# First feed-forward block in one pass over 512 rows, hidden squares kept on chip, low weight parts written over their ring slots

## The reference

```python
D_MODEL, SEQ, CTX_LEN, MLP_HIDDEN = 1024, 256, 256, 4096

def squared_relu_mlp(h, w1, w2):
    return jnp.square(jax.nn.relu(h @ w1)) @ w2

for i in range(DEPTH):                     # DEPTH == 2
    ...
    x = x + gt1 * y_lat
    x = x + gt2 * squared_relu_mlp(modulate_2(rms_norm(x, norm2_g[i]), sh2, sc2), mlp_w1[i], mlp_w2[i])
    if not last:
        ctx = ctx + mods_c[2] * y_ctx
        ctx = ctx + mods_c[5] * squared_relu_mlp(modulate_2(rms_norm(ctx, norm2_g[i]), mods_c[3], mods_c[4]),
                                                 mlp_w1[i], mlp_w2[i])
```

## Time and profile before

| | us |
|---|---|
| median of 3 runs | 2895.1 (2892.4 to 2897.35) |
| span of the profiled execution | 2890.3 |
| PE busy | 2770.7 (96%) |
| PE weight loads busy | 1973.5 (68%) |
| DVE busy | 1186.3 (41%) |
| ACT busy | 709.9 (25%) |

### The profile page before, as it was taken

The page is one execution under the profiler, slowest core; times in us unless marked ns, Lnnn a source line. Parts: engine busy times, 40 slices in busy tenths (PEclk is TensorE's granted clock), DMA queues, the critical chain, the costliest instruction groups (busy, mean ns, idle before and its releaser), DMA issues.

```text
span 2890.3 us, 49935 instructions
## 1 busy us (share of the span) xinstructions
PE 2770.7 (96%) x22276; PEld 1973.5 (68%) x22276; DVE 1186.3 (41%) x2055; ACT 709.9 (25%) x1136; POOL 48.3 (2%) x39
## 2 busy tenths in 40 slices
PE   8899999999999999999998999999999999998998
PEld 6788997877533333333332756899999965697998
DVE  4667764332301101101101587356555433553554
ACT  2234333131200000000000214334444322211443
POOL 0000000000000000000000000000000000131000
PEclk9899999999999999999999999999999998999999
DMA  8756765544899999999999225265554330010452
GB/s 334 304 182 260 277 259 204 190 175 150 347 373 421 421 420 421 420 421 420 421 412 421 74 97 193 73 262 204 190 182 160 140 117 15 24 54 24 181 184 80
DMA packets 95198, 686.88 MB, mean 238 GB/s; under 512 B 10624, under 2 KB 11776, under 8 KB 11904
## 3 DMA queue, kind: packets, MB, share of 16 engines
q1 hardware_dynamic: 94400, 681.37, 60.5%
q10 hardware_dynamic: 576, 2.25, 0.2%
HBM read 682.52 MB, written 1.05 MB: 237 GB/s over the span
## 4 chain that ended last, share of the span: by engine, by line
PE 86%; DMA 6%; DVE 5%; ACT 2%; issue 1%; SPq 0%; POOL 0%; ACTq 0%; DVEq 0%
PE ps L530 42%; PE ps L2053 15%; PE ps L890 12%; PE ps L801 6%; PE ps L2078 5%; DMA AR<-W 3%; DMA ring<-W 2%; PE ps L543 2%; PE ps L2081 2%; PE ps L776 1%; PE ps L2061 1%; DVE macc L646 0%; DMA XT<-XIN 0%; SPq L3577 0%; ACT AR L1761 0%
## 5 line engine op out<-in xcount | busy, mean ns | idle before, releaser
L2053 PE MATMUL ps<-AR 128*32 128x512 f32 x2904 | 440.1, 593 | 11.6 <-DMA AR<-W 10.2
L530 PE MATMUL ps<-HT,ring 128*128 128x256 f32 (+1 forms) x1696 | 443.4, 422 | 1.7 <-ACT HT L719 1.7
L530 PEld LDWEIGHTS ps<-HT,ring 128*128 128x128 f32 x1696 | 324.2, 193 | 114.5 <-issue 75.0
L530 PE MATMUL ps<-FR,FR 128*128 128x256 f32 x3120 | 387.4, 284 | 0.0
L530 PEld LDWEIGHTS ps<-FR,FR 128*128 128x128 f32 x3120 | 378.7, 192 | 3.0 <-issue 2.9
L872 DVE TENSOR_TENSOR FR<-ring,FR 128x2048 fp32r<-128x2048 f32 x129 | 294.4, 2291 | 164.4 <-ACT FR L856 164.4
L890 PE MATMUL ps<-FR,FR 128*128 128x256 f32 x2832 | 349.0, 283 | 0.0
L890 PEld LDWEIGHTS ps<-FR,FR 128*128 128x128 f32 x2832 | 343.8, 192 | 0.0
L2173 DVE TENSOR_TENSOR AR<-AR,ps 128x256 f32<-128x256 f32 x70 | 29.6, 423 | 678.9 <-ACT AR L2136 361.0
L2053 PE MATMUL ps<-ring,AR 128*32 128x512 f32 x1576 | 288.8, 594 | 5.8 <-DMA ring<-W 3.5
L856 ACT ACTIVATE FR<-ring 128x2048 fp32r<-128x2048 f32 x129 | 244.7, 1908 | 130.9 <-PE ps L890 85.2
(11 more groups left out here) (430 smaller groups left out, 2517.1 us busy)
## 6 DMA issues: line engine op xcount, KB each, us to landing
ring<-W SPq DMA_DIRECT2D x431, 1024.0 KB, 5.8
AR<-W SPq DMA_DIRECT2D x215, 1024.0 KB, 21.0
XT<-XIN ACTq DMA_DIRECT2D x2, 1024.0 KB, 8.7
cst<-CS SPq DMA_DIRECT2D x1, 1859.0 KB, 14.3
out<-XT SPq DMA_DIRECT2D x4, 256.0 KB, 2.2
sml<-SM SPq DMA_DIRECT2D x1, 970.5 KB, 10.3
cst<-CS ACTq DMA_DIRECT2D x1, 129.5 KB, 8.1
sml<-SM ACTq DMA_DIRECT2D x1, 16.0 KB, 5.7
```

The source lines that it names most:

```text
L530: ins = g.matmul(out, l, r, **kw)
L2053: ins = g.matmul(bank.ap[group(i), :], mo.hg[e % 2][:, 4 * h + k, group(t)], w[n][:, k, :], start=j == 0 and k == 0, stop=j == 1 and k == ...
```

## The change

The stage no longer goes twice over the weights. `wide_pe` does all 16 slots of w1 for both halves, then all 16 slots of w2, and each slot is loaded and split once: `SLOTS` falls from 646 to 614. A matmul has 512 columns instead of 256, except in slots 0 and 1, which are used for the latent half first and, after the context norm, for the context half. All squares of the hidden layer stay on chip (`wi.H`, 32 tiles of 128 x 512; their low parts overwrite them, `H_low`, and the high parts pass through five turning buffers). The sums of w2 take all 8 PSUM banks. In the last two slots of w2 PE goes bank by bank over both slots, and DVE adds each bank to `XT` as it comes.

`InPlace` replaces `Splits` here: two buffers hold the high part of a slot (`parts = 2`), and the low part is written over the slot in its ring place (`ring_low` is the ring's memory, seen as fp32r). The place is freed by PE's last matmul on the slot (`used`), no longer by DVE. The 9 background steps stand behind slots 2 to 10 of w1. The norm for `odd_mixer` comes after the whole stage. The second feed-forward (`m1`) is written in a form of its own with the same instructions.

```diff
@@ schedule()
-def early_step(block, c, r):
-    return 1 if block == 0 and c == 0 and r < 23 - ATTENTION_STEPS else 0
+def wide_steps(n):
+    return 1 if 2 <= n < 25 - ATTENTION_STEPS else 0
...
     load("ev_out", 4)
-    for block in range(2):
...
-        for c in range(2 - block):
-            for n in range(17):
-                if n < 16:
-                    ahead(2)
-                if n:
-                    ahead(2)
-                bg.go(early_step(block, c, n))
+    load("m0_1", 2)
+    for n in range(16):
+        load("m0_1" if n < 14 else "m0_2")
+        bg.go(wide_steps(n))
+    load("m0_2", 14)
...
@@ program()
+        class InPlace(Splits):
+            def __init__(self, x, names, fr, get):
+                self.x, self.names, self.parts, self.get = x, names, 2, get
...
+            def pair(self, i):
+                return self.hi[:, i % 2, :], ring_low[:, where[slot(*self.names[i])][0], :]
+            def make_dve(self, g, s, n):
...
+                    s.wait_ge(self.x + ".hi", i)
+                    g.tensor_tensor(low, src, high.bitcast(F32), SUB).then_inc(*s.done(self.x + ".lo", i))
...
-        def mlp_pe(g, s, q, bg):
...
+        def wide_pe(g, s, bg):
...
+            def used(n):
+                return s.done("m0.used", n, frees=(slot(*wi.names[n]),))
+            latent, context = slice(0, 256), slice(256, 512)
+            up(0, latent, 0)
+            down_end("ev.down1")
+            up(1, latent)
+            norm_pe(g, s, "m0", (1,))
+            for n in range(2):
+                up(n, context, 1 if n == 0 else None).then_inc(*used(n))
+            for n in range(2, 16):
+                up(n, slice(0, 512)).then_inc(*used(n))
+                bg.go(wide_steps(n))
+            acc = [counts.take("m0.down", m, keep=True) for m in range(8)]
+            for i in range(14):
+                s.wait_ge("m0.lo", 16 + i).wait_ge("m0.d_lo", i)
+                for kk in range(2):
+                    for m in range(8):
+                        if i + kk == 0:
+                            s.wait_emptied(acc[m])
+                        ins = down(i, kk, m)
+                ins.then_inc(*used(16 + i))
+            for i in (14, 15):
+                s.wait_ge("m0.lo", 16 + i).wait_ge("m0.d_lo", i)
+            for m in range(8):
+                for i in (14, 15):
+                    for kk in range(2):
+                        ins = down(i, kk, m)
+                ins.then_inc(*s.done("m0.bank", m, frees=(slot("m0_2", 14), slot("m0_2", 15)) if m == 7 else ()))
...
+            norm_pe(g, s, "odd")
+        def wide_act(g, s):
...
+            for n in range(16):
+                s.wait_ge("m0.used", n)
+                for h in range(2):
+                    g.activation(wi.H[:, 2 * n + h, :], counts.bank("m0.up", n, h)[:, :], ACT.Relu).then_inc(
+                        *s.done("m0.relu", n, h, empties=("m0.up", n, h)))
+                w.make_act(g, s, n + 3)
...
+            for i in range(16):
+                w.make_act(g, s, min(16 + i + 3, 32))
+                if i + 3 < 16:
+                    hidden(i + 3)
+            s.mark("m0.end")
+            squares_act(g, s, "odd", odd_ready(s), 0)
+            norm_root_act(g, s, "odd", 0)
+            shift_act(g, s, "odd", MN["ada1"][0], 0)
```

More of the change, by code:

```diff
@@ L17 @@
 SLOT = 2048
-SLOTS = 646
+SLOTS = 614
 RING = 5
@@ L455, in program @@
         XT = sb("XT", [128, 2, 8, 256])
+        with ExitStack() as first:
+            HT_low = first.enter_context(nc.sbuf_tensor("HT_low", [128, 8, 512], F32R))
         HT = sb("HT", [128, 8, 512])
@@ new lines, in program, with mlp_pe @@
+        ml.pairs = tuple(x[:, :].rearrange("p (k t) -> p k t", k=8) for x in ml.HS)
+        def mlp_pe(g, s):
+            norm_pe(g, s, "m1")
+            w = Splits("m1", ml.names, ml.fr, PARTS, from_ring)
+            for n in range(17):
+                if n < 16:
+                    i = w.next()
+                    b = counts.take("m1.up", n)
+                    s.wait_emptied(b).wait_ge("m1.lo", i)
+                    if n == 0:
+                        up3_by_k(g, s, "m1", 0, ml.pairs, [
+                            (w.pair(i), 0, b.ap[:, 0:256], True, None),
+                            (w.pair(i), 128, b.ap[:, 256:512], False, lambda: s.done("m1.used", i))])
+                    else:
+                        for h in range(2):
+                            ins = up3(g, w.pair(i), ml.pairs, h * 128, b.ap[:, h * 256:h * 256 + 256])
+                        ins.then_inc(*s.done("m1.used", i))
+                if n == 1:
+                    acc = [counts.take("m1.down0", k, keep=True) for k in range(4)]
+                if n:
+                    i = w.next()
+                    s.wait_ge("m1.lo", i).wait_ge("m1.d_lo", n - 1)
+                    down3(g, s, "m1.down0", w.pair(i), n - 1, 16, acc, [x[:, (n - 1) % 3, :, :] for x in ml.d]).then_inc(*s.done("m1.used", i))
+            down_end("m1.down0")
+            s.mark("m1.end")
@@ new lines, in mlp_act @@
+        def mlp_act(g, s):
+            w = Splits("m1", ml.names, ml.fr, PARTS, from_ring)
+            w.make_act(g, s, 3)
+            norm_act(g, s, "m1", lambda h, k: s.wait_ge("res", "od.down", k))
+            shift_act(g, s, "m1", MN["ada1"][0], 24, ml.pairs[0])
+            for n in range(17):
+                if n < 16:
+                    w.act(g, s, 2)
+                    s.wait_ge("m1.used", ml.at["m1_1", n])
+                    if n >= 2:
+                        s.wait_ge("m1.d_lo", n - 2)
+                    g.activation(ml.hid[n % 2], pair2(counts.bank("m1.up", n)), ACT.Relu).then_inc(*s.done("m1.relu", n, empties=("m1.up", n)))
+                    s.wait_ge("m1.hid", n)
+                    if n >= 3:
+                        s.wait_ge("m1.used", ml.at["m1_2", n - 3])
+                    g.activation(ml.d[0][:, n % 3, :, :], ml.hid[n % 2], ACT.Copy).then_inc(*s.done("m1.d_hi", n))
+                if n:
+                    w.act(g, s, 2)
+            s.mark("m1.end")
@@ L2857, in odd_pe @@
             both("od.in", 1)
-            down_end("m0.down1")
             both("od.in", 2)
```

290 lines of the change are left out of this document (153 added, 137 removed).

## The result

| | before | changed |
|---|---|---|
| median of the runs | 2893.75 us (2887.31 to 2897.35, 4 runs) | 2946.48 us (2943.88 to 2949.21, 4 runs) |
| span of the profiled execution | 2890.3 us | 2947.2 us |
| stage, first matmul to the 0.64 us one of the mixer | 388.5 us | 437.8 us |
| the same, to the mixer's second group of products | 399.5 us | 457.2 us |
| mean granted clock of the program | 0.976 | 0.966 |

The changed kernel is slower by 1.85%: ratio 1.0185, 95% interval [1.0172, 1.0197], +52.7 us between the medians, +56.9 between the profiled spans. The forecast was 2922.7 us, +27.6, with a range of 2902 to 2956. The sign and the range were right; the size was half. The last but one line of the table (from 1884.78 to 2284.31 us before, from 1884.47 to 2341.65 after) is the measure used from here on. I call it the stage time.

A forecast was written before the change was run, and what follows sets the result against it. The prediction took PE's own work to bound the stage, busy 388 of 388 us at full clock. Terms -31.1 + 39.0 + 6.5 + 5.7 + 7.5 = +27.6 us on 2895.1 gave 2922.7 us, range 2902 to 2956.

The forecast's parts named there:

- matmuls, made wide: Slots of w1 and w2: 1440 matmuls of 512 columns at 218.4 ns replace 2880 narrow ones, 31.1 us saved.
- six ada1 waits, with clock: Background steps using ada1 slots 18 to 23: PE waits 4.8 us for each late transfer, 6.5 with clock, 39.0 in all.
- wait at slot 15: Last two slots of w2: PE waits 4.8 us for the low part of slot 15, 6.5 us with clock.
- context norm: Norm before the context half, with only two narrow units of PE work ahead: costs 5.7 us, clock included.
- norm for the next mixer: After the whole stage, no longer covered: wait 5.8 us plus clock 1.7, together 7.5 us.
- rival with two narrow prices: Wide matmuls of w1 and w2: each costs two narrow ones, 240 ns, giving 2953.8 us; chance 0.09.
- the tenth step loads nothing: Background steps in w1: the tenth loads no ada1 slot, so no transfer wait was counted for it.
- slots in time: Background steps in w1: rival where ada1 transfers start early enough, the six waits vanish, giving 2883.7 us; chance 0.07.
- 1.7 us a wait: Low granted clock behind each PE wait over 4 us: costs 1.7 us, ends 0 and 2.7.
- rival in which the clock stays low: Slots behind the six ada1 waits run wholly at 1.2 GHz, 8.8 us more each, 2975 us; chance 0.05.
- main case: Whole kernel: the summed forecast of 2922.7 us, covering 2909 to 2940 with single terms moved; chance 0.77.
- rival in which a wide matmul costs as much as a narrow one: Wide matmuls of w1 and w2: weight loads alone set the pace, 120 ns each, giving 2781 us; chance 0.02.

The follow-up runs named there:

- e8: Changed kernel with ada1 slots first, last background step first on DVE, context norm sooner and latent columns first in the last two down slots; median 2875.14 us, ratio 0.995.
- e1: Changed kernel with each ada1 slot loaded ahead of the m0 weight slot it stood behind; stage time 416.2 us, ratio 1.006 to the kernel before.
- e4: Changed kernel with only the last down slot, not the last two, worked bank by bank; stage time 449.7 us, ratio 1.0173 to the kernel before.
- e5: Changed kernel with the context norm's spread matmuls ahead of the latent columns of up slot 1; stage time 450.2 us, ratio 1.0176 to the kernel before.
- e6: Changed kernel with latent columns of the last two down slots first and the next mixer's norm started after the second context bank; stage time 441.9 us, ratio 1.0129.
- e2: Changed kernel with the last background step on DVE ahead of the squares of up slot 10; stage time 447.4 us, ratio 1.0172 to the kernel before.
- e7: Changed kernel with some down slots cut to 384, 256 or 128 columns, leaving work out; 175.4, 117.9 and 110.6 ns a matmul, 232.1 at 512.
- e3: Changed kernel with every 512-column matmul of up and down split into two of 256; stage time 464.0 us, ratio 1.0219 to the kernel before.
- e9: Changed kernel with 18 unused float32 matmuls of 256 columns ahead of each of six late ada1 products; stage time 463.8 us, ratio 1.0214.
- e11: Changed kernel with 9 unused float32 matmuls of 256 columns ahead of each of six late ada1 products; stage time 443.5 us, ratio 1.0158.
- e12: Changed kernel with some down slots reading bfloat16, leaving work out; 226.9 ns for fp32r control and four-byte steps together, 216 ns for columns side by side.
- e10: Changed kernel with one of the three products done three times in some down slots, leaving work out; 48 matmuls took 11.19 us (low weights), 10.88 and 10.89 (high).

## Why the forecast was right in sign and half in size

With the waits gone the stage is 11.9 us shorter than before, and the waits with their clock are worth 69.6 us. 69.6 - 11.9 = 57.7, the whole difference in stage time. The forecast had 58.7 - 31.1 = 27.6. Point by point:

| step of the forecast | forecast | measured | from |
|---|---|---|---|
| matmuls, made wide | -31.1 | -11.9 | e8 against before |
| six ada1 waits, with clock | +39.0 | +41.0 | e1 |
| wait at slot 15 | +6.5 | +7.5 | e4 |
| context norm | +5.7 | +7.0 | e5 |
| norm for the next mixer | +7.5 | +7.8 | e6 less e4 |
| bank of the finished sums | none | +9.8 | e2 |

The last five singly make 73.1, against 69.6 together. The difference of 3.5 us is, to 0.3, the 2.3 us in e2 and the 1.5 in e5 that lie at other waits; without them the bank cost 7.5 and the context norm 5.5, where 5.7 was forecast.

**Wide matmuls: the term that was mis-sized.** 19 of the 30 us missed are here. The step reasoned that the 13 ns of a narrow fp32r matmul beyond its columns were a weight load uncovered, and that a float32 matmul, 218.4 ns and 430 ns for twice the columns, showed the price with the load covered. The mechanism was the wrong one. In the changed arrangement the price is nearly all columns, narrow or wide: 0.446 ns each at 256 and above (e7), where the clock allows 0.417. A further 2.2 ns of the narrow 120 went with the arrangement and not with the width (e3), and make about half of the 11.9 us. The float32 rows take two clocks a column (218.4 ns for 256, and e9 shows that a float32 matmul is two such passes); they could not show the price of an operand that is wanted once each clock. (So the 430 ns for 512 columns, which the forecast took for both passes, are one of them.) The rival with two narrow prices (240 ns) was nearer to the 231 than my 218.4, and the forecast's own test, "I am wrong if 48 wide matmuls take 11 us or more", was met: 11.1.

**The tenth wait: a step left out.** I followed the freed ring places and not the freed PSUM banks. The step said "the tenth step loads nothing" (it is the ninth of the nine in this stage) and took it to cost nothing; but it is the one that empties a bank, and it had moved to stand behind PE's own newest work. Up slots have two banks each and turn, and slot 11 meets the bank of the finished sums.

**The waits for ada1 slots: right.** Six, 4.43 to 4.56 us each where 4.8 were forecast, 18.7 to 20.1 us apart where 16 to 17 were (the forecast's own terms, 10.5 + 1.4 + 4.8 + 1.7, give 18.4), the clock 0.50 for a while behind each. e1 shows the cause given, the position in the ring. The rival "slots in time" is refuted by the six waits; e1 is what that rival would have been, by one line of order.

**The clock: undersized.** 1.7 us a wait forecast, 2.2 measured (e11). The 1.7 came from 8.84 against 7.15 us, and there, as behind the wait of 4.15 us, the low stretch was one of the short ones: 3.5 us, over well before the 32 matmuls were. Here only two of the six were short. The 2.7 us end of the range, from the row of the 5.38 us wait, was as near. The rival in which the clock stays low is refuted: 1.00 again for the rest of each slot.

**Slot 15 and the two norms: right**, 22.3 us against 19.7, or 20.8 with 5.5 for the context norm.

**That the range held** owes something to its width: its upper part was there for the rival of doubled matmuls, and the time came there by three terms together, the matmuls, the clock and the wait left out. The 2909 to 2940 given for the main case did not hold it, and single terms moved as listed would have reached only 2935.

**The rule weighed in the forecast.** The rival in which a wide matmul costs as much as a narrow one, 120 ns, is refuted by 231 ns. The Trainium skill (TensorE: Matmul & The Clock Gate, Back-to-back issue gap) gives about 131 ns for a sustained 512-column matmul with its load. The runs do not agree; the lowest 512-column price in the runs here is 216 ns, with bfloat16 (e12).

## What to carry to other kernels

A buffer that is now freed by the matmul that reads it, and not by the split before it, must be handed on to a transfer that is wanted at least one slot later: look for the pair of "frees" and "needs" that stand next to each other, and swap the order of the loads. Do the same for PSUM banks: a small step that empties a bank belongs ahead of the big work on its engine that waits for PE. And price a wide matmul from rows of the same data type; the width saved some 7 us here and all changes to the matmuls together 12, less than a fifth of what ten unnoticed or accepted waits cost.

## What the runs showed of the hardware

- In the changed kernel's arrangement fp32r matmuls of 256 to 512 columns cost 0.446 ns a column plus 4 ns at a granted clock of 1.00, and 128 columns 111 ns (e7). At clock 0.50 behind a wait, wide ones start 0.43 us apart (2076.05 and 2076.48 above), which is 512 / 1.2 GHz = 427 ns with hardly any surplus. Bfloat16 side by side has hardly any either (216 ns beside 213.3), and in steps of four bytes has the same as fp32r (e12). Together these speak for a limit on four-byte columns of some 0.44 ns that the clock does not move; that is an inference from the three, not measured by itself.
- The same 256-column product cost 120.0 ns in the kernel before and 117.8 ns in the arrangement of the changed one (e3). This stays unexplained.
- Low weights, written in place, cost 233 ns against 227 for high ones (e10). This stays unexplained too.
- The granted clock fell to 0.50 at the end of each wait of 4.06 to 5.63 us, up to 1.6 us before PE's next matmul or just behind it, and stayed there for some 3.5 us (three waits) or nearly 7 us (seven). With 0.5 us of waiting in place of 4.5, it did not fall in these steps at all (e11).
